# Encoder-layer kernel: the output weights' split moved partly ahead, the hand-off loads reordered, and all weight sums on VectorE

## The chip, the cores and the metric

One Trainium2 chip, of which the kernel uses one core. The metric is the device time of one execution in microseconds (us), lower is better. The trace and the profile come from one profiled execution; all times inside it count from the start of its span.

## The reference, cut to what matters

One encoder layer in float32 on x of 2048 x 1024: an RMS norm, one input projection (1024 to 2304 columns), two kinds of attention, an output projection with a residual, a SwiGLU feed-forward block, a final norm. The change touches the projection, the preparation of the output projection's weights and the start of the attention:

```python
h = rmsnorm(x, g_norm_mix[l])
proj = h @ w_in[l]                       # q, k, v of both kinds of attention
...
oa = neighbourhood_attention(qa, ka, va, na_rpb[l])
ob = windowed_gqa_sink(qb, kb, vb, swa_sink[l])
o = concatenate([rmsnorm(oa, g_out_na[l]), rmsnorm(ob, g_out_swa[l])])
x = x + o @ w_out[l]
```

## The kernel before, in words

**Precision.** A float32 factor is split into two rounded parts, hi (ScalarE, a cast) and lo (VectorE, the value less its hi), and a product is made of three matmuls: hi times hi, hi times lo, lo times hi. Weights and operands must be split before TensorE can use them.

**Stages.** First the tokens are normed and turned and the first 512 value columns are made (up to 116 us). Then comes the product stage, on which the change works: the remaining columns, by a scheme with seven products for a 2 x 2 block product. The tokens are taken in two halves (b = 0, 1) and each half in seven groups of 256 columns; so there are 14 runs g of seven products j, 98 products n = 7g + j, each of 12 matmuls (`product`, L883, lines 910 to 912). The seven operands of the second half (`proj_h_second`, 1 MB each) lie in HBM as sums and are loaded (`load_op`, L315) and split (L563, L729) before run 7.

**Step n.** ScalarE, VectorE and SyncE (SP, which issues most DMAs) each go through steps n = 0 to 99 in a fixed order, written out in tables of steps; each engine works strictly in order, so a wait holds all that is behind it. ScalarE in step n first waits for product n and copies it out where j is 0, 2, 3 (`evacuate`, L577, copy at L590), casts the weights of product n + 6 into a ring of six slots (`pair_hi`, L575), casts an operand where `SPLIT_AT` (L169) says so, then casts finished results into one of three stages (`result_hi`, L602, cast at L618), which first waits for the store that used that stage before. VectorE in step n adds the copied part to the product (`join`, L736, at j = 1, 4, 5), makes the lo parts of the results of step n - 1 (`result_lo`, L775 and L777), turns four results of run 1 and of run 8 by the rotary tables (`rope`, four operations each), makes the lo part of the weight pair (L733) and of the operand (L729). TensorE reads a product's bank pairs by the rules at L883: products j = 2, 4, 5 need ScalarE's copies, j = 6 needs the join of j = 4. Four times (around products 19, 22, 68 and 71) TensorE also turns value results (L880, four transposes each).

**Weight sums.** Each run needs four sums or differences of weight blocks (L453, L455, L459, L464). For runs 1 to 5 VectorE makes them, in steps of the run before (`SUMS_AT` puts the first two of run 1 in step 2); for runs 6 to 13 GpSimd (POOL) does, between its own weight loads (`load_raw`, L466).

**Output weights.** The eight blocks k of `w_out` (512 KB each) are loaded into one buffer (`load_out_weights`), scaled by the group norms' gains and cast (L626, ScalarE), their lo part is made (L782, VectorE), and both parts are stored to HBM (L366, 1 MB). Before, block k is loaded in step 53 + 5k, split in step 55 + 5k and stored after that. The load of block k + 1 waits for the split of block k, since there is one buffer, and the split waits for the store of the block before.

**Operand loads.** In SP's list operand 1 is loaded in step 8 and operand 0 in step 23; they are split in steps 26 and 33. Operands 2 to 6 are loaded by ScalarE's queue in steps 42 to 46.

**Hand-off.** The attention starts with head pair 0 of the neighbourhood kind. Its units u (two heads for each of 16 tiles of queries) go through TensorE (score, L1301; turn, L1313; values, L1336), VectorE (L1248, L1261) and ScalarE (exp, L1200; copy, L1222). Scores 0 to 7 need query portion q0 and key portions k0 and k1; score 8 needs q1 and k2. SP issues q0 in step 91, k0 and k1 in step 93, values v0 and v1 in step 94, the last two mask loads in step 97, and only after the last result's store k2, q1 and the rest (`later_loads`). The results of the last run are numbered r = 52 to 55; r = 55 uses the same stage as r = 52. ScalarE copies no turned unit before the store of r = 53 has landed (`last_stage_stored`, L264). GpSimd makes the bias tables (L1178): kind 0 from masks and `rel` ahead of the hand-off, kinds 1 and 2 once all results are split.

**Banks.** Runs with odd g use PSUM banks 3, 4, 5 (`bank_of`, L178), and the product j = 6 of run 13 ends in bank 3, which the attention's score 3 needs.

The lines quoted are these; the result i of run g is finished in step 7g + `HI_AT`, or 7g + (3, 5, 6, 7) for the runs that it does not name:

```python
    OP_LOADS = {8: 1, 23: 0}
    SPLIT_AT = {26: (1, 1), 33: (1, 0), 46: (1, 2), 48: (1, 3), 49: (1, 4), 51: (1, 5), 52: (1, 6)}
    SUMS_BY_POOL, SUMS_AT = range(6, G), {1: 2}
    HI_AT = {ROPED: (3, 6, 7, 9), VALUES: (3, 7, 6, 9)}
    ROPE_AT = (2, 5, 6, 8)
    OUT_AT = {53 + 5 * k: k for k in range(KT)}
```

## Time and profile before

| | |
|---|---|
| Time, median of 3 runs | 2212.57 us (2206.57 to 2215.93) |
| Profiled execution: its own time | 2212.51 us |
| Profiled execution: span | 2210.7 us |
| Mean granted TensorE clock | 0.992 |
| TensorE (PE) busy | 2147.3 us, 97% |
| VectorE (DVE) busy | 1563.0 us, 71% |
| ScalarE (ACT) busy | 1013.1 us, 46% |
| GpSimd (POOL) busy | 296.1 us, 13% |

The product stage is the stretch from 116.4 to 407.6 us. The shares are means over the whole span; TensorE is near its full share in all stages after 470 us, which this change leaves as they are. Matmuls are pipelined: one shows 0.39 us where the next starts 0.23 us later, so starts say more than durations.

### The profile page before, as it was taken

To read this page: it belongs to the slowest core of one execution; us is meant where nothing else is said; L and a number is where in the kernel's file an instruction comes from. 1 tells how busy PE (TensorE), PEld (TensorE's weight loads), DVE (VectorE), ACT (ScalarE), POOL (GpSimd) and SP (SyncE) were. 2 spreads that over 40 slices of the span, in tenths; PEclk is the share of its full clock that TensorE was granted. 3 is DMA by queue.
4 is the path that set the end of the run, shared out by engine and by line. 5 is a ranking of instruction groups with operands and counts; after the bars stand their busy time and mean duration, and the time that the engine had idled before them with its cause. 6 is when DMAs were issued, how large, how long until landed. Compare 5 with 4: busy or idle time off the path is not lost.

```text
span 2210.7 us, 33085 instructions
## 1 busy us (share of the span) xinstructions
PE 2147.3 (97%) x11168; PEld 1774.7 (80%) x11168; DVE 1563.0 (71%) x2860; ACT 1013.1 (46%) x1967; POOL 296.1 (13%) x307
## 2 busy tenths in 40 slices
PE   7999989699999999999999999999999999999998
PEld 6878767588888888878888888888888887888887
DVE  6776775489888787786656568765656578575676
ACT  5645544388899634353333335333333334131343
POOL 2343432445100000011121211100000000000000
PEclk9999999899999999999999999999999999999999
DMA  6776868999964376565464548332332386353544
GB/s 211 258 236 210 287 216 271 258 265 244 218 195 133 117 237 238 195 223 201 143 213 149 197 165 316 136 124 91 107 108 82 111 321 216 115 185 101 191 148 155
DMA packets 267750, 419.34 MB, mean 190 GB/s; under 512 B 15434, under 2 KB 157266, under 8 KB 261088
## 3 DMA queue, kind: packets, MB, share of 16 engines
q1 hardware_dynamic: 253664, 371.91, 52.3%
q0 software_dynamic: 10240, 30.48, 4.6%
q10 hardware_dynamic: 3712, 15.21, 2.0%
q8 instruction: 79, 1.29, 0.2%
q14 instruction: 55, 0.45, 0.1%
HBM read 264.70 MB, written 156.04 MB: 190 GB/s over the span
## 4 chain that ended last, share of the span: by engine, by line
PE 84%; DVE 6%; DMA 5%; issue 2%; SPq 2%; ACT 1%; DVEq 0%; ACTq 0%
PE late_psum L2393 12%; PE late_psum L2395 12%; PE late_psum L2394 12%; PE late_psum L2419 6%; PE late_psum L2420 6%; PE late_psum L2421 6%; PE late_psum L1336 4%; PE late_psum L1313 3%; PE late_psum L1735 2%; PE late_psum L1737 2%; PE late_psum L1736 2%; PE late_psum L910 2%; PE late_psum L912 2%; PE late_psum L911 2%; PE late_psum L1301 2%
## 5 line engine op out<-in xcount | busy, mean ns | idle before, releaser
L2393 PE MATMUL late_psum<-ff_h,ff_ring 128*128 128x512 f32 x1232 | 479.8, 389 | 1.6 <-DVE ff_acts L2254 1.4
L2394 PE MATMUL late_psum<-ff_h,ff_ring 128*128 128x512 f32 x1232 | 479.3, 389 | 0.0
L2395 PE MATMUL late_psum<-ff_h,ff_ring 128*128 128x512 f32 x1232 | 479.3, 389 | 0.0
L2393 PEld LDWEIGHTS late_psum<-ff_h,ff_ring 128*128 128x128 f32 x1232 | 231.3, 188 | 50.7 <-DVE ff_acts L2254 2.3
L2395 PEld LDWEIGHTS late_psum<-ff_h,ff_ring 128*128 128x128 f32 x1232 | 231.3, 188 | 48.2
L2394 PEld LDWEIGHTS late_psum<-ff_h,ff_ring 128*128 128x128 f32 x1232 | 231.3, 188 | 48.0
L2419 PE MATMUL late_psum<-ff_d,ff_a 128*128 128x512 f32 x616 | 240.1, 390 | 2.1 <-DVE ff_x L2312 1.4
L2421 PE MATMUL late_psum<-ff_d,ff_a 128*128 128x512 f32 x616 | 239.7, 389 | 0.0
L2420 PE MATMUL late_psum<-ff_d,ff_a 128*128 128x512 f32 x616 | 239.7, 389 | 0.0
L2312 DVE TENSOR_TENSOR ff_x<-late_psum,ff_x 128x512 f32<-128x512 f32 x224 | 153.3, 690 | 116.4 <-PE late_psum L2421 115.5
L2212 DVE TENSOR_TENSOR ff_ring<-ff_raw,ff_ring 128x512 fp32r<-128x512 f32 x176 | 131.8, 750 | 99.4 <-ACT ff_ring L2089 99.3
L2104 ACT CAST ff_a<-ff_a 128x768 fp32r<-128x768 f32 (+2 forms) x96 | 81.6, 878 | 206.7 <-DMA ff_a<-acts_scratch 206.5
L2212 DVE TENSOR_TENSOR ff_ring<-ff_sums,ff_ring 128x512 fp32r<-128x512 f32 x132 | 96.1, 729 | 111.6 <-ACT ff_ring L2089 111.2
L2089 ACT CAST ff_ring<-ff_raw 128x512 fp32r<-128x512 f32 x176 | 109.3, 623 | 136.4 <-PE late_psum L2395 135.4
L1200 ACT ACTIVATE att_probs<-att_neg_scores,att_negmax 128x385 f32<-128x385 f32 (+4 forms) x256 | 161.1, 629 | 20.6 <-DVE att_negmax L1248 19.6
L1313 PE MATMUL late_psum<-ident,att_probs 128*128 128x128 f32 (+1 forms) x816 | 133.9, 277 | 8.5 <-ACT att_probs_turned L1222 4.5
L2419 PEld LDWEIGHTS late_psum<-ff_d,ff_a 128*128 128x128 f32 x616 | 115.6, 188 | 27.9 <-issue 2.1
L1222 ACT COPY att_probs_turned<-late_psum 128x384 f32<-128x384 f32 (+2 forms) x256 | 124.5, 487 | 27.1 <-PE late_psum L1313 27.0
L2420 PEld LDWEIGHTS late_psum<-ff_d,ff_a 128*128 128x128 f32 x616 | 115.6, 188 | 23.9
L2421 PEld LDWEIGHTS late_psum<-ff_d,ff_a 128*128 128x128 f32 x616 | 115.6, 188 | 23.8
L2089 ACT CAST ff_ring<-ff_sums 128x512 fp32r<-128x512 f32 x132 | 81.4, 618 | 113.5 <-PE late_psum L2395 110.2
L1301 PE MATMUL late_psum<-att_k_stack,att_q_stack 128*128 128x384 f32 (+3 forms) x256 | 113.0, 441 | 16.5 <-DMA att_q_stack<-qk_scratch 7.7
(208 smaller groups left out, 4142.9 us busy)
## 6 DMA issues: line engine op xcount, KB each, us to landing
acts_scratch<-ff_acts SPq DMA_DIRECT2D x22, 1792.0 KB, 7.7
ff_a<-acts_scratch SPq DMA_DIRECT2D x24, 960.0 KB, 5.1
ff_raw<-in_w_gate SPq DMA_DIRECT2D x44, 512.0 KB, 3.8
ff_raw<-in_w_up SPq DMA_DIRECT2D x44, 512.0 KB, 3.9
att_q_stack<-qk_scratch SPq DMA_DIRECT2D x64, 256.0 KB, 6.4
ff_d<-down_scratch SPq DMA_DIRECT2D x21, 768.0 KB, 6.5
proj_raw<-in_w_in POOLq DMA_DIRECT2D x14, 1024.0 KB, 9.5
ffn_in_scratch<-mix_h_stage SPq DMA_DIRECT2D x8, 1792.0 KB, 6.3
```

What stands on the lines that cost most here:

```text
L1200: nc.scalar.activation(pr[:, i, lo:hi], sn[:, i, lo:hi], ACT.Exp, bias=negmax[:, i:i + 1], scale=-1.0, accum_out=total[:, i:i + 1]).then_i ...
L1301: pe.matmul(out, q, kind.keys(k_st[:, e, 0, :], t), start=True, stop=False)
L1313: last = pe.transpose(tp[0:rows, u % 2, j * P:(j + 1) * P], pr[:, i, c0 + j * P:c0 + j * P + rows], ident[:])
L2089: nc.scalar.copy(ff.ring[m % TURNS][:, 0], weight_of(m)).then_inc(w_hi_done, 1)
L2212: nc.vector.tensor_tensor(ff.ring[m % TURNS][:, 1], weight_of(m), ff.ring[m % TURNS][:, 0], ALU.subtract) \
L2312: nc.vector.tensor_tensor(to, down_bank(e, j), to, ALU.add).then_inc(added, 1)
L2393: pe.matmul(out_bank, whi[:, k], hhi[:, :, k], start=(k == 0 and not onto), stop=False, skip_group_check=onto)
L2394: pe.matmul(out_bank, whi[:, k], hlo[:, :, k], start=False, stop=False, skip_group_check=onto)
L2395: last = pe.matmul(out_bank, wlo[:, k], hhi[:, :, k], start=False, stop=(k == 3), skip_group_check=onto)
L2419: pe.matmul(bank, hi, dhi, start=(i == 0 and not onto), stop=False, skip_group_check=onto)
L2420: pe.matmul(bank, hi, dlo, start=False, stop=False, skip_group_check=onto)
L2421: last = pe.matmul(bank, lo, dhi, start=False, stop=(i == n - 1), skip_group_check=onto)
```

## The change

- The output weights are split in two groups of four. Blocks 0 to 3 are loaded in steps 14, 15, 19, 25, split in steps 18, 23, 28, 32; blocks 4 to 7 are loaded in steps 51, 53, 58, 63 and split in steps 57, 62, 67, 72. Each half has two raw buffers and one buffer for the parts. The first half's buffers lie in the home of operand 1, so that operand's load moves from step 8 to step 36 and waits for the fourth store; its split moves from step 26 to step 40. Operand 0's load moves from step 23 to step 21.
- All weight sums are made by VectorE. The first two of run 1 move to step 4, the third to step 5, and weight pairs 7 to 12 each come one step later.
- Odd runs use banks 5, 4, 3 where they used 3, 4, 5; score 3 now waits for the last join, and turn 1 for the last result.
- Results r = 52 and 53 get two stages of their own, in the buffer of the weights of even runs.
- The masks and `rel` are loaded in steps 77 to 85. In the hand-off SP issues q0 in step 92, k1 in step 94, v0 and v1 in step 95, k2 and q1 in step 96; ScalarE's queue issues k0 in step 93. v2, k3, q2, q3 and v3 stay behind the last store.

```diff
@@ -161,22 +162,22 @@
         return hs[:, o] if t >= 8 else op_sums(0, o)[:, quarter(t)]
-    SPLIT_ORDER = [(0, o) for o in (2, 3, 4, 6)] + [(1, o) for o in (1, 0, 2, 3, 4, 5, 6)]
-    OP_LOADS = {8: 1, 23: 0}
+    SPLIT_ORDER = [(0, o) for o in (2, 3, 4, 6)] + [(1, o) for o in range(SEVEN)]
+    OP_LOADS = {21: 0, 36: 1}
     LATE_OPS, OP_SLOTS = PER_G * HALF_GROUPS - PER_G - 2, range(2, SEVEN)
...
     PAIR_AT_TILE = {11: 0, 12: 1, 13: 2}
-    SPLIT_AT = {26: (1, 1), 33: (1, 0), 46: (1, 2), 48: (1, 3), 49: (1, 4), 51: (1, 5), 52: (1, 6)}
-    SUMS_BY_POOL, SUMS_AT = range(6, G), {1: 2}
+    SPLIT_AT = {33: (1, 0), 40: (1, 1), 46: (1, 2), 48: (1, 3), 49: (1, 4), 51: (1, 5), 52: (1, 6)}
+    SUMS_BY_POOL, SUMS_AT = (), {1: 4}
     PAIRS_AT = {n: (n + RING,) for n in range(PRODUCTS - RING)}
-    PAIRS_AT.update({0: (4, 5, 6), 1: (), 2: (), 3: (7,), 4: (8, 9), 5: (10, 11)})
+    PAIRS_AT.update({0: (4, 5, 6), 1: (), 2: (), 3: (), 4: (7, 8), 5: (9, 10), 6: (11, 12)})
     HOME_FREED = {o: PER_G * HALF_GROUPS - PER_G + o - 1 for o in range(2, SEVEN)}
...
     def bank_of(g, j):
-        return ps[:, 3 * (g % 2) + BANK_OF[j]]
+        return ps[:, 5 - BANK_OF[j] if g % 2 else BANK_OF[j]]
     def weight_of(n):
...
@@ -216,6 +218,10 @@
...
         stored_by[r] = (stored_by[r - STAGES] if r >= STAGES else 0) + (16 if is_value(g, i) else 32)
+    def stage_of(r):
+
+        return {LAST_RUN: STAGES, LAST_RUN + 1: STAGES + 1}.get(r, r % STAGES)
+
     def results_at(n):
...
@@ -247,10 +253,13 @@
...
         else:
+            eng.wait_ge(summed, 3 * G)
+
+    def turns_free(eng, u):
+        if u == 0:
+            eng.wait_ge(summed, 3 * G)
+        else:
             eng.wait_ge(res_lo, LOWS)
-
-    def turns_free(eng):
-        eng.wait_ge(summed, 3 * G)
     def last_turn_read(eng):
...
@@ -317,6 +323,8 @@
...
             eng.wait_ge(h_stored, 128)
+            if o == 1:
+                eng.wait_ge(out_stored, 64)
         if o == 0:
...
@@ -346,51 +354,71 @@
...
                 to = qk_dram[part, r0:r0 + P, cols]
-            sp.dma_start(to, src).then_inc(stored[slot], 16)
+            sp.dma_start(to, src).then_inc(landed, 16)
     def load_out_weights(k):
         if k == 0:
+            sp.wait_ge(parts_stored, 128)
+            sp.wait_ge(h_stored, 128)
+        elif k in (4, 5):
             sp.wait_ge(prod_done, PER_G * HALF_GROUPS)
-        else:
-            sp.wait_ge(out_lo_done, k)
+        elif k >= 2:
+            sp.wait_ge(out_lo_done, k - 1)
+        raw_rows = out_raw[k // 4][k % 2]
         if k < 4:
-            sp.dma_start(out_raw[:], w_out[k * P:(k + 1) * P, :]).then_inc(out_in, 32)
+            sp.dma_start(raw_rows[:], w_out[k * P:(k + 1) * P, :]).then_inc(out_in[k % 2], 32)
             return
...
             r0 = AW + (k - 4 + 4 * e) * HD
-            sp.dma_start(out_raw[e * HD:(e + 1) * HD, :], w_out[r0:r0 + HD, :]).then_inc(out_in, 16)
+            sp.dma_start(raw_rows[e * HD:(e + 1) * HD, :], w_out[r0:r0 + HD, :]).then_inc(out_in[k % 2], 16)
     def store_out_weights(k):
         sp.wait_ge(out_lo_done, k + 1)
-        sp.dma_start(out_dram[k], out_parts[:].bitcast(F32)).then_inc(out_stored, 16)
-
-    OUT_AT = {53 + 5 * k: k for k in range(KT)}
+        sp.dma_start(out_dram[k], out_parts[k // 4][:].bitcast(F32)).then_inc(out_stored, 16)
+
+    OUT_LOAD_AT = {14: 0, 15: 1, 19: 2, 25: 3, 51: 4, 53: 5, 58: 6, 63: 7}
+    OUT_AT = {18: 0, 23: 1, 28: 2, 32: 3, 57: 4, 62: 5, 67: 6, 72: 7}
+
+    NEAR_AT = {77: 3, 79: 4, 81: 0, 83: 1, 85: 2}
     def load_near(part):
+        if part == 3:
+            out_weights_stored(sp)
+        if part == 0:
+            sp.wait_ge(roped, 8)
+            sp.wait_ge(v_turned, 4)
+            sp.wait_ge(table_made, 16 * (2 + 8 * NAH))
         dst, src = near_parts[part]
-        sp.dma_start(dst, src).then_inc(near_in if part < 3 else near_masks_in, 16)
+        sp.dma_start(dst, src).then_inc(near_in, 16)
+
+    FIRST_AT = {92: 0, 94: 2, 95: 3, 96: 4}
     def first_loads(att, turn):
-        sp.wait_ge(prod_done, PRODUCTS - SEVEN + (1, 3, 4)[turn])
+        eng = act if turn == 1 else sp
+        eng.wait_ge(prod_done, PRODUCTS - SEVEN + (1, 3, 3, 4, 4)[turn])
         if turn == 0:
...
         if turn == 1:
-            att.load_k(att.near, 0, 0)
+            for slot in range(STAGES):
+                act.wait_ge(stored[slot], max(v for r, v in stored_by.items() if r % STAGES == slot and order[r][1] < G - 2))
+            att.load_k(att.near, 0, 0, act)
+        if turn == 2:
             att.load_k(att.near, 0, 1)
-        if turn == 2:
+        if turn == 3:
             for half in range(2):
...
             att.load_v(att.near, 0, 1)
+        if turn == 4:
+            att.load_k(att.near, 0, 2)
+            att.load_q(att.near, 0, 1)
     def later_loads(att):
-        att.load_k(att.near, 0, 2)
-        att.load_q(att.near, 0, 1)
         att.load_v(att.near, 0, 2)
...
@@ -416,29 +444,16 @@
...
                 load_op(sp, OP_LOADS[n])
-            if n in OUT_AT:
-                load_out_weights(OUT_AT[n])
-            if n - 2 in OUT_AT:
-                store_out_weights(OUT_AT[n - 2])
-            if n == 78:
-                sp.wait_ge(roped, 8)
-                sp.wait_ge(v_turned, 4)
-                sp.wait_ge(table_made, 16 * (2 + 8 * NAH))
-                load_near(0)
-            if n in (83, 87):
-                load_near({83: 1, 87: 2}[n])
+            if n in OUT_LOAD_AT:
+                load_out_weights(OUT_LOAD_AT[n])
+            if n - 1 in OUT_AT:
+                store_out_weights(OUT_AT[n - 1])
+            if n in NEAR_AT:
+                load_near(NEAR_AT[n])
+            if n in FIRST_AT:
+                first_loads(att, FIRST_AT[n])
             for r, g, i in results_at(n - 1):
                 store_result(r, g, i)
-            if n == 91:
-                first_loads(att, 0)
-            if n == 93:
-                first_loads(att, 1)
-            if n == 94:
-                first_loads(att, 2)
-            if n == 97:
-                out_weights_stored(sp)
-                for part in (3, 4):
-                    load_near(part)
         later_loads(att)
...
@@ -600,10 +615,12 @@
...
     def result_hi(r, g, i):
-        slot, kind = r % STAGES, res_kind(g, i)
-        if r >= STAGES:
-            act.wait_ge(stored[slot], stored_by[r - STAGES])
-        elif slot == 2:
+        slot, kind = stage_of(r), res_kind(g, i)
+        if STAGES <= r < LAST_RUN + STAGES:
+            act.wait_ge(stored[r % STAGES], stored_by[r - STAGES])
+        if r == LAST_RUN:
+            act.wait_ge(w_lo_done, PER_G * (G - 1))
+        if r == 2:
             for half in range(2):
...
@@ -620,12 +637,12 @@
...
             act.wait_ge(gains_in, 48)
-        act.wait_ge(out_in, 32 * (k + 1))
+        act.wait_ge(out_in[k % 2], 32 * (k // 2 + 1))
         if k >= 1:
             act.wait_ge(out_stored, 16 * k)
-        nc.scalar.mul(out_parts[:, 0], out_raw[:], gains[:, k:k + 1]).then_inc(out_hi_done, 1)
-
-    def scalar():
+        nc.scalar.mul(out_parts[k // 4][:, 0], out_raw[k // 4][k % 2][:], gains[:, k:k + 1]).then_inc(out_hi_done, 1)
+
+    def scalar(att):
         load_x(0)
...
@@ -831,12 +851,12 @@
...
                     first_weight_sums(dve, g + 1)
-                if j == 2:
+                if n == (5 if g == 0 else PER_G * g + 2):
                     middle_weight_sum(dve, g + 1)
...
                     last_weight_sum(dve, g + 1)
-            if n - 2 in OUT_AT:
-                out_weights_lo(OUT_AT[n - 2])
+            if n in OUT_AT:
+                out_weights_lo(OUT_AT[n])
     def turn_tile(n):
...
@@ -1304,8 +1324,8 @@
...
         c0, _, _ = kind.score_cols(t)
-        if u == 0 and isinstance(r, int) and r == 0:
-            proj.turns_free(pe)
+        if u < 2 and isinstance(r, int) and r == 0:
+            proj.turns_free(pe, u)
         pe.wait_ge(probs_done, UNITS * r + u + 1)
...
@@ -1409,7 +1429,7 @@
...
         self.p_sums = self.at("proj_w_sums", 207872, [P, 2, 4, P])
-        stages = (24576, 28672, 180224)
+        stages = (24576, 28672, 180224, 199680, 203776)
         self.p_st_hi = [self.at(f"stage_hi{i}", off, [P, BANK], F32R) for i, off in enumerate(stages)]
...
@@ -1417,8 +1437,9 @@
...
         self.p_spare = [self.at(f"proj_spare{b}", off, [P, BANK]) for b, off in enumerate((75776, 55296))]
-        self.p_out_raw = self.at("w_out_raw", 32768, [P, D])
-        self.p_out_parts = self.at("w_out_parts", 36864, [P, 2, D], F32R)
+        self.p_out_raw = [[self.at(f"w_out_raw{half}_{i}", off, [P, D]) for i, off in enumerate(offs)]
+                          for half, offs in enumerate(((81920, 94208), (32768, 61440)))]
+        self.p_out_parts = [self.at(f"w_out_parts{half}", off, [P, 2, D], F32R) for half, off in enumerate((86016, 36864))]
         self.ident = self.at("ident", self.IDENT, [P, P])
```

## Rows read from the trace of the kernel before

**Rows 1.** Busy by stretch: length, busy PE PEld DVE ACT POOL (instructions), PEclk, DMA share, GB/s

```profile
116.44:407.60 291.16, 274.82 (x1193) 223.21 (x1191) 195.12 (x264) 131.79 (x213) 109.94 (x119) 0.98 0.76 244
...
407.60:431.46 23.86, 7.12 (x25) 5.67 (x26) 9.54 (x31) 8.92 (x22) 10.03 (x9) 0.67 1.05 293
...
137.46:164.66 27.20, 27.20 (x122) 22.52 (x120) 23.83 (x42) 10.10 (x18) 9.79 (x17) 1.00 0.72 230
```

**Rows 2.** Timeline of TensorE: first matmuls of six products: start, us, engine, line

```profile
116.44 0.39 PE L910 MATMUL late_psum<-proj_h_first,proj_ring 128*128 128x512 f32 x1
...
119.16 0.39 PE L910 MATMUL late_psum<-proj_h_first,proj_ring 128*128 128x512 f32 x1
...
134.62 0.47 PE L910 MATMUL late_psum<-proj_h_first_last,proj_ring 128*128 128x512 f32 x1 [1.70 <-issue]
...
269.66 0.50 PE L910 MATMUL late_psum<-proj_h_second,proj_ring 128*128 128x512 f32 x1 [1.59 <-DVE proj_h_second L729]
...
307.19 0.80 PE L910 MATMUL late_psum<-proj_h_second,proj_ring 128*128 128x512 f32 x1 [6.59 <-ACT proj_c L590]
...
365.08 0.79 PE L910 MATMUL late_psum<-proj_h_second,proj_ring 128*128 128x512 f32 x1 [2.51 <-DVE proj_c L742]
```

**Rows 3.** Chain of waits, products 19 to 21: start us, us, what

```profile
173.73 0.44 PE late_psum L880 x4
```

**Rows 4.** Waits, 237 to 408 us: who waited for what: total us, times, longest

```profile
ACT w_out_parts L626 <- DMA w_out_raw<-in_w_out: 17.0, 5, 9.7
...
ACT stage_hi L618 <- DMA qk_scratch<-stage_lo: 8.5, 4, 6.8
```

**Rows 5.** Chain of waits from the last product to the ninth score

```profile
408.80 8.20 DMA qk_scratch<-stage_lo
...
417.02 0.61 ACT stage_hi L618
...
424.05 7.18 DMA att_q_stack<-qk_scratch
...
431.46 0.76 PE late_psum L1301
```

**Rows 6.** Timeline around the hand-off: SP's queue, VectorE, GpSimd and ScalarE

```profile
399.05 5.54 SPq L1107 DMA_DIRECT2D att_k_stack<-qk_scratch  x8
...
418.26 0.51 DVE L1248 CUSTOM_DVE_ANT_0 att_neg_scores<-late_psum,bias 128x352 f32<-128x352 f32 x1
...
419.61 3.75 SPq L1107 DMA_DIRECT2D att_k_stack<-qk_scratch  x4
...
421.43 13.62 POOL L1178 TENSOR_TENSOR bias<-near_mask,rel 128x512 f32<-128x512 f32 x12 [25.48 <-DMA near_mask<-in_na_mask]
...
423.53 0.59 ACT L1200 ACTIVATE att_probs<-att_neg_scores,att_negmax 128x352 f32<-128x352 f32 x1 [0.44 <-DVE att_negmax L1248]
...
432.81 0.66 DVE L1248 CUSTOM_DVE_ANT_0 att_neg_scores<-late_psum,bias 128x480 f32<-128x480 f32 x1 [5.85 <-PE late_psum L1302]
```

**Rows 7.** VectorE's groups: by tile, 116 to 200, 237 to 408, 116 to 408 us

```profile
L729 DVE TENSOR_TENSOR proj_h_second<-proj_h_second x7: 2278/2292/3244, 196.3 to 270.1; 128x2048 fp32r<-128x2048 f32 x7
...
L733 DVE TENSOR_TENSOR proj_ring<-proj_raw,proj_ring 128x512 fp32r<-128x512 f32 x17 | 11.6, 687 | 4.5 <-ACT proj_ring L575 4.5
...
L733 DVE TENSOR_TENSOR proj_ring<-proj_raw,proj_ring 128x512 fp32r<-128x512 f32 x29 | 27.7, 966 | 8.0 <-ACT proj_ring L575 8.0
...
L782 DVE SCALAR_TENSOR_TENSOR w_out_parts<-w_out_raw,g_out,w_out_parts 128x1024 fp32r<-128x1024 f32 x8 | 10.3, 1293 | 22.0 <-ACT w_out_parts L626 22.0
...
L464 DVE TENSOR_TENSOR proj_w_sums<-proj_raw,proj_w_sums 128x512 f32<-128x512 f32 x6 | 4.1, 686 | 0.0
```

**Rows 8.** DMA times to landing: second-half operand loads, then output-weight stores

```profile
DMA to landing us min/median/max: 6.1/10.9/14.0
...
DMA to landing us min/median/max: 3.9/5.3/12.1
```

**Rows 9.** DMA traffic from 392 to 442 us

```profile
DMA packets 8887, 13.48 MB, mean 270 GB/s; under 512 B 681, under 2 KB 4137, under 8 KB 8758
```

More of the change, by code:

```diff
@@ L781, in out_weights_lo @@
         dve.wait_ge(out_hi_done, k + 1)
[L782 to L783 removed]
+        parts = out_parts[k // 4]
+        nc.vector.scalar_tensor_tensor(out=parts[:, 1], in0=out_raw[k // 4][k % 2][:], scalar=gains[:, k:k + 1],
+                                       in1=parts[:, 0], op0=ALU.mult, op1=ALU.subtract).then_inc(out_lo_done, 1)
     def vector():
```

35 lines of the change are left out of this document (17 added, 18 removed).

## The prediction

> **What bounds the kernel now.** I read busy time by stretch first [rows 1]. In the product stage (116.44 to 407.60 us) TensorE shows 274.82 us busy of 291.16, in the 23.86 us after it only 7.12. So the change works in two places in which TensorE does wait. How much is lost in the first? Two undisturbed products start 2.72 us apart (116.44 and 119.16) [rows 2]; 98 of them are 266.6 us, and four turns of values at 0.44 us [rows 3] are 1.8. So 291.2 - 266.6 - 1.8 = 22.8 us of the product stage are stall. Its large pieces [rows 2]: product 6 starts at 134.62 where 116.44 + 6 x 2.72 = 132.76 was due; product 54 waits 1.59 for VectorE's operand part; product 65 waits 6.59 for ScalarE's copy and product 83 waits 2.51 for VectorE's join. Both resume at half the clock (0.80 and 0.79 us for a matmul, where 0.39 is usual), which makes them dearer than the idle alone.
>
> Who holds ScalarE and VectorE? ScalarE waited 17.0 us for the output weights' loads, 9.7 the longest, and 8.5 us for stores out of the result stages [rows 4]; the 9.7 is the wait that ends just ahead of product 65. In the hand-off the chain runs over a stage store of 8.20 us from 408.80 (r = 52, whose stage r = 55 wants), the last result's hi part at 417.02, then SP's later issues and q1's landing of 7.18 us, to score 8 at 431.46 [rows 5], 23.9 us after the product stage.
>
> **First part: output weights, steps 14 to 72.** Each load now starts four to nine steps ahead of its split (11 to 24 us) where it was two steps (5.4 us). The longest wait now comes 9.7 us on top of those 5.4, so a load needs up to 15 us; the tightest of the second half (step 51 for 57) has 16, and block 0's (step 14 for 18) has some 19, since SP has nothing to issue in steps 12 and 13 and comes to it early. I take the waits behind products 65 and 83 as gone, and with them the small ones that follow a late ScalarE. In the first half the same four splits are new work: 4 x 1.29 us on VectorE [rows 7], where TensorE ran without a gap from 137.46 to 164.66 with VectorE 23.83 of 27.20 us busy [rows 1]; the later steps 18 to 32 have no rotary work, so I cost them at nothing. If that cover is gone the price is 5.2 us.
>
> Operand 1's load is the delicate move. Its issue waits in SP's list for the fourth store. Let product 33 start at P. The fourth split ends at P + 2.5 and its store lands 5.3 us later, 12.1 at most [rows 8]; step 36 itself comes at about P + 10. So the load goes out at P + 10 to P + 15 and takes 10.9 us (6.1 to 14.0) [rows 8]: P + 16 to P + 28.6, likeliest P + 21. Its split comes up at P + 21.8 (step 40). The next copy that TensorE needs from ScalarE is product 42's, due at P + 29.9, with 3.1 us of work before it. So 5 us of lateness cost nothing, and the worst case loses 2. Operand 0's load in step 21 waits for the value turn after product 22 as it did, and now holds the stores of steps 20 and 21 behind it; ScalarE meets that in step 24, after its copies of that run: nothing, or 2 us.
>
> **Second part: weight sums on VectorE.** GpSimd's operations stretch VectorE's: the weights' lo part took 0.687 us up to 200 us and 0.966 from 237 to 408, 29 times, 8.1 us in all; an operand part took 3.24 instead of 2.29 [rows 7]. That ends. In exchange VectorE gets 32 operations of 0.69 us [rows 7], 22 us over eight runs of 19 us. Is there room? The stretch of 27.20 us has 42 instructions in 23.83 us busy, four of them empty, so 0.63 each. A run needs 3 joins, 4 lo parts, 7 pairs and 4 sums, 18 x 0.63 = 11.3 us. Over steps 42 to 69 (76.2 us) that is 45.4, with five operand parts 11.5, four rotary turns 10.1 and three output parts 3.9: 70.9 us, 93%. It fits on the whole, not in steps 46 to 52, where 11.3 + 11.5 = 22.8 us meet 19.0. Laid out step by step, VectorE ends operand 6's part and the join of product 53 some 7 us after product 53's start, and product 55 is due 5.4 after it; product 54 is 0.4 late. So products 54 and 55 lose 2.0 us, where product 54's idle alone is 1.59 now. In the rotary steps 58 to 64 the same layout has VectorE some 5 us behind its steps, with the join for product 69 just late: 0.8.
>
> **Third part: start of the product stage.** VectorE sat in the sums of run 1 until the weights landed, with the join for product 6 behind it. Moved to step 4, the join goes first: 1.9 us back.
>
> The product stage: 22.8 us of stall, of which I leave 2.0 + 0.8 and 2.5 for landings (operand loads, stage stores of the first half): 5.3. **Gain 17.5 us**, between 8 (all the new costs above) and 22.
>
> **Fourth part: hand-off.** Call the stage's end T. With two more stages r = 55 waits for no store: its parts are made by T + 1.3, and scoring can start, given k1. SP issues k1 when product 93 is done, T - 10.9; four issues took 2.8 us (half of 5.54 [rows 6]) and a landing 7 to 8 us [rows 5], so about T. Units 0 to 7 took VectorE from 418.26 to 432.81 less 5.85 idle, 8.7 us [rows 6], so unit 8 could be shifted at T + 10.2; it was at T + 25.2. GpSimd's bias kind 1 is the first half of 13.62 us [rows 6] and starts at about T + 1.5: no later than that. But ScalarE waits for r = 53's store before unit 0's copy and exp 5, and SP now issues k2 and q1 (3.75 us for k2 [rows 6]) ahead of it. Bytes bound this: 13.48 MB went at 270 GB/s from 392 to 442 us [rows 9]. From T - 15 to that store there are four stores, q0, k0, k1, v0, v1, k2, q1 and r = 53: 6.75 MB, 25 us, so T + 10 if nothing pauses. I take T + 11. From exp 5 to unit 8's shift the trace has 9.28 us with 5.85 idle [rows 6], 3.4; unit 8 at T + 14.4. **Gain 11 us**, between 4 and 15.
>
> The rule that speaks against this part is in the Trainium skill, DMA: Bandwidth & Descriptors, Issuing engines are not separate DMA queues: transfers from all engines run on the same 16 DMA engines, so k0 on ScalarE's queue would save issue time only. By that rule the sum would count 2.8 us of issue for k0 and nothing for its landing.
>
> **Sum.** 2212.51 (the profiled execution, as good as the median 2212.57) - 17.5 - 11 = 2184.0 us. All later stages only move, since TensorE, VectorE and ScalarE meet the same work in the same order there.
>
> **Rivals.** (a) The hand-off is bound by transfers: the DMA share is 1.05 there [rows 1], and packing the same bytes closer makes each landing longer: with pauses before the loads of T - 10.9 and T - 8.2, the 25 us count from T - 6, and unit 8 comes at T + 22. Then 3 us are gained: 2192. For it speaks the full share; against it, that the masks and the last output-weight store (2.3 MB, 8.6 us at 270 GB/s) leave the stretch. (b) VectorE bounds steps 42 to 69: at its records' 0.69 us instead of 0.63, the 88 short operations there take 5.3 us more and fill the 76.2 us, and two stalls with half-clock restarts add some 3. Then the stage gains 8 us less: 2192. Against it speaks the full 27.20 us at 88% busy. (c) Slower: ScalarE, in order, now meets loads in the first half where it met none, four output-weight blocks and two operands. One such wait of 9.7 us cost product 65 some 8 us (6.59 idle and matmuls at half the clock). It decides from the fourth wait of that length on; all six cost 49 us and give 2212.5 + 49 - 28.5 = 2233. Against it: 15 us and more from issue to want for the blocks, 12 for the operands. (d) Both (a) and (b), or the gains are given back at once: 2202 to 2212.
>
> **Chances.** Forecast 0.60, (a) 0.16, (b) 0.14, (c) 0.03, (d) 0.07. A measurement of this kernel can tell about 0.5%, 11 us. Faster by more: 0.60 + 0.16 + 0.14 and 0.01 of (d), 0.91; within 0.5%: the other 0.06 of (d); slower: 0.03. The range takes the forecast's bounds (12 to 37 us of gain, 2175 to 2200) and both single rivals: 2174 to 2200.
>
> **What would show it.** Right: no wait of ScalarE for output weights, product 65 on time, the weights' lo part back at 0.69 us, TensorE's product stage near 274 us long, unit 8 shifted 13 to 16 us after it, last result's hi part within 1 us of the last product. Wrong: ScalarE waiting at step 18 or 40 for a load; TensorE idle for VectorE's joins in products 54 to 69 by more than 4 us; score 8 or 16 waiting for q1, k2 or q2 beyond T + 15. A span above 2200 would make the prediction wrong.

## The result, and the profile after

| | before | after |
|---|---|---|
| Time, median of 4 runs | 2212.31 us | 2198.21 us (2197.29 to 2200.47) |
| Ratio | | 0.994, 95% interval 0.9917 to 0.9963 |
| Profiled execution: its own time | 2212.51 us | 2197.36 us |
| Profiled execution: span | 2210.7 us | 2195.2 us |
| End of the product stage (T) | 407.4 us | 400.3 us |
| From T to the end | 1803.3 us | 1795.0 us |

The change gains 14.1 us where 28.5 were forecast. The time lies inside the range, but the gain is half of the forecast. T is read here as 0.23 us after the start of the last product's last matmul. The last two lines of the table split the 15.5 us between the two profiled executions: 7.1 us in the product stage (forecast 17.5) and 8.3 us behind it (forecast 11).

Busy time by stretch of the changed kernel: the product stage, the 23.86 us after it, and the first runs [rows 1].

```profile
116.01:400.25 284.24, 274.45 (x1193) 224.87 (x1191) 203.18 (x296) 131.83 (x212) 57.24 (x87) 0.98 0.80 257
400.25:424.11 23.86, 14.72 (x101) 11.71 (x102) 16.57 (x56) 15.19 (x39) 13.66 (x12) 0.79 1.08 277
136.00:163.20 27.20, 27.20 (x122) 22.53 (x121) 25.19 (x44) 11.79 (x21) 10.36 (x18) 1.00 0.73 218
```

The stage is 284.2 us long, so by the prediction's own count 284.2 - 266.6 - 1.8 = 15.8 us of stall are left, where 5.3 were forecast. TensorE does twice as much as before in the 23.86 us after it.

TensorE's timeline, first matmuls of product 30 (203.35), 51 (266.72) and 65 (308.98) of the changed kernel:

```profile
203.35 0.80 PE L930 MATMUL late_psum<-proj_h_first,proj_ring 128*128 128x512 f32 x1 [4.60 <-ACT proj_c L605]
...
266.72 0.63 PE L930 MATMUL late_psum<-proj_h_second,proj_ring 128*128 128x512 f32 x1 [3.39 <-issue]
...
308.98 0.50 PE L930 MATMUL late_psum<-proj_h_second,proj_ring 128*128 128x512 f32 x1 [0.19 <-ACT proj_c L605]
```

Product 65 is on time, as forecast, and so are 6 and 83. But two products that ran without a gap before are now late. "Loss" from here on is the time by which the matmuls of a product start later than one per 0.227 us: the gap ahead of it plus its slow matmuls, read from the starts. Product 30 loses 4.8 + 2.4 us and its successor 0.3, product 51 loses 3.6 + 1.7: 12.7 us in all. That is more than the 10.5 us by which the stall exceeds the 5.3 that the forecast left; the 3.1 us of stall besides it are less than 5.3.

Waits of ScalarE from 110 to 402 us, changed kernel, then the same row of the kernel before:

```profile
ACT stage_hi L635 <- DMA qk_scratch<-stage_lo: 25.8, 8, 11.5
```

```profile
ACT stage_hi L618 <- DMA qk_scratch<-stage_lo: 13.5, 6, 6.8
```

No wait for an output weight's load is left, and 0.8 us of wait for an output weight's store [rows 4]. The wait for a stage's store has doubled instead, and one of them is 11.5 us long. ScalarE and the chain of waits around it, changed kernel:

```profile
197.84 0.63 ACT L635 ACTIVATE stage_hi<-proj_c 128x512 fp32r<-128x512 f32 x1 [11.49 <-DMA qk_scratch<-stage_lo]
...
202.73 0.56 ACT L605 COPY proj_c<-late_psum 128x512 f32<-128x512 f32 x1
```

```profile
180.77 17.05 DMA qk_scratch<-stage_lo
...
197.84 0.64 ACT stage_hi L635
```

A store of 256 KB issued at 180.77 took 17.05 us to land. ScalarE stood at L635 for it, with the copy for product 30 behind it in its order.

The hand-off [rows 5, 6]: the chain that leads to score 16, then ScalarE and VectorE.

```profile
407.39 4.86 SPq L1127
...
415.79 12.64 DMA att_q_stack<-qk_scratch
...
428.54 0.48 PE late_psum L1321
```

```profile
413.68 0.48 ACT L1242 COPY att_probs_turned<-late_psum 128x384 f32<-128x384 f32 x1 [5.83 <-DMA qk_scratch<-stage_lo]
...
416.44 0.63 DVE L1268 CUSTOM_DVE_ANT_0 att_neg_scores<-late_psum,bias 128x480 f32<-128x480 f32 x1
```

ScalarE's first copy waits for r = 53's store, until T + 13.4 (forecast T + 11). Unit u is timed by the start of its first VectorE operation, in which its scores are shifted (L1268). Unit 8 is shifted at T + 16.2 (forecast T + 14.4, before T + 25.4). Unit 16 comes at T + 29.2, because score 16 needs q2, whose last part SP issues at 415.79 and which takes 12.64 us to land, at T + 28.2. The prediction had named this as a sign of being wrong: "score 8 or 16 waiting for q1, k2 or q2 beyond T + 15".

VectorE's groups, changed kernel, weight lo parts (L752) from 237 to 400 us and one kind of weight sum [rows 7]:

```profile
L752 DVE TENSOR_TENSOR proj_ring<-proj_raw,proj_ring 128x512 fp32r<-128x512 f32 x30 | 21.3, 714 | 12.5 <-ACT proj_ring L590 12.5
...
L468 DVE TENSOR_TENSOR proj_w_sums<-proj_raw 128x512 f32<-128x512 f32 x9 | 6.2, 686 | 0.0
```

The lo part is back at 0.71 us from 0.97.

### The profile page after: what moved, and what is told of

It is laid out like the page before. It is cut to its first block, busy times and chain, and to the rows that moved or that the text cites. A ratio compares the mean times of both kernels' runs of the same rounds, so it can differ in the third digit from the quotient of the medians.

```text
span 2195.2 us, 33087 instructions
## 1 busy us (share of the span) xinstructions
PE 2144.0 (98%) x11168; PEld 1775.8 (81%) x11168; DVE 1569.1 (71%) x2892; ACT 1012.1 (46%) x1967; POOL 245.0 (11%) x275
## 4 chain that ended last, share of the span: by engine, by line
PE 86%; DVE 5%; DMA 4%; issue 2%; ACT 1%; SPq 1%; DVEq 0%; ACTq 0%
PE late_psum L2414 12%; PE late_psum L2415 12%; PE late_psum L2416 12%; PE late_psum L2440 6%; PE late_psum L2442 6%; PE late_psum L2441 6%; PE late_psum L1356 4%; PE late_psum L1333 3%; PE late_psum L930 3%; PE late_psum L932 3%; PE late_psum L931 3%; PE late_psum L1756 3%; PE late_psum L1758 3%; PE late_psum L1757 3%; PE late_psum L1321 2%
## 5 line engine op out<-in xcount | busy, mean ns | idle before, releaser
L2233 DVE TENSOR_TENSOR ff_ring<-ff_raw,ff_ring 128x512 fp32r<-128x512 f32 x176 | 131.1, 746 | 102.4 <-ACT ff_ring L2110 102.3
L1220 ACT ACTIVATE att_probs<-att_neg_scores,att_negmax 128x385 f32<-128x385 f32 (+4 forms) x256 | 161.2, 630 | 19.6 <-DVE att_negmax L1268 18.8
L1333 PEld LDWEIGHTS late_psum<-ident,att_probs 128*128 128x128 f32 (+1 forms) x816 | 98.4, 139 | 43.5 <-issue 24.8
```

Of the source, the lines that this page charges most:

```text
L1220: nc.scalar.activation(pr[:, i, lo:hi], sn[:, i, lo:hi], ACT.Exp, bias=negmax[:, i:i + 1], scale=-1.0, accum_out=total[:, i:i + 1]).then_i ...
L1333: last = pe.transpose(tp[0:rows, u % 2, j * P:(j + 1) * P], pr[:, i, c0 + j * P:c0 + j * P + rows], ident[:])
L2233: nc.vector.tensor_tensor(ff.ring[m % TURNS][:, 1], weight_of(m), ff.ring[m % TURNS][:, 0], ALU.subtract) \
```

## The experiments

Each edit is to the changed kernel unless it says otherwise. Single executions are compared by their stages in the trace; kernels with the changed hand-off differ by up to 5 us from T to the end (1792 to 1797), so differences below that are not read as effects there. Nor are small differences in time: except where a median is given each time is of one execution, and the kernel before took 2210.48 us beside the first four edits, 2208.31 beside the next four, 2209.6 (median of nine) beside the three after them and 2209.97 beside the last two.

**Operand 0's load later.**

```diff
-    OP_LOADS = {21: 0, 36: 1}
+    OP_LOADS = {23: 0, 36: 1}
```

> The changed kernel with operand 0's load back in step 23. In the changed kernel's trace product 30 stands still for 4.8 us and restarts at half the clock (7.1 us lost in all), behind a result store of step 20 that took 17 us to land: SP had held it until product 22's value turn and then issued it just behind the 1 MB operand load. Theory A (order in SP's list): the store goes out in step 21 again, ahead of the load, the stall at product 30 is gone, and the time falls by about 7 us, to some 2191. Theory B (the output weights' new traffic in the first half slows the stores whatever the order): the stall stays within 2 us of what it is, the time stays at 2198.

2199.94 us. Product 30 still loses 5.3 + 1.8 us, product 51 still 6.4. A place two steps later in SP's list does not remove the first stall (Theory B). ScalarE's timeline now has other, shorter waits for stores ahead of it:

```profile
195.04 0.63 ACT L635 ACTIVATE stage_hi<-proj_c 128x512 fp32r<-128x512 f32 x1 [7.87 <-DMA qk_scratch<-stage_lo]
...
202.73 0.63 ACT L635 ACTIVATE stage_hi<-proj_c 128x512 fp32r<-128x512 f32 x1 [3.23 <-DMA v_window_scratch<-stage_values]
```

The second of them is released just before the copy at 203.27, and it waits for a value store. So the lateness is not one store's alone.

**Operand 1's split one step earlier.**

```diff
-    OP_LOADS = {21: 0, 36: 1}
-    SPLIT_AT = {33: (1, 0), 40: (1, 1), ...
+    OP_LOADS = {23: 0, 36: 1}
+    SPLIT_AT = {33: (1, 0), 39: (1, 1), ...
```

> As the run before, and operand 1 split in step 39 instead of 40. The changed kernel loses 5.2 us at product 51, where ScalarE waits for stores of steps 41 and 42 that were issued among the five operand loads of steps 42 to 46 and took 16 to 18 us to land. Theory A (the operand split in step 40, 1.9 us on ScalarE and 2.3 on VectorE, pushes those stores behind the loads): stores of steps 40 and 41 go out some 2 us earlier and the loss at product 51 falls by 2 us or more; time some 3 to 5 us under the run before, about 2187. Theory B (VectorE is late there from the weight sums, or the loads alone fill the transfer engines): the loss at product 51 changes by less than 1 us.

2196.12 us. Product 51 loses 0.1 where it lost 5.2, product 30 still loses 6.3, products 54 and 55 lose 3.8 instead of 2.1. T is 396.7. The stall goes as Theory A says; the time does not reach its 2187, which counted on a smaller stall at product 30. So product 51's stall hangs on the split in step 40. The changed kernel's SP shows how:

```profile
234.84 0.33 SPq L357 DMA_DIRECT2D qk_scratch<-stage_hi  x1
...
242.24 0.33 SPq L357 DMA_DIRECT2D qk_scratch<-stage_hi  x1
...
247.48 0.45 SPq L357 DMA_DIRECT2D qk_scratch<-stage_lo  x1
```

and its ScalarE queue and ScalarE:

```profile
241.87 0.35 ACTq L334 DMA_DIRECT2D proj_h_second<-proj_in_scratch  x1
...
259.88 0.63 ACT L635 ACTIVATE stage_hi<-proj_c 128x512 fp32r<-128x512 f32 x1 [3.96 <-DMA qk_scratch<-stage_lo]
...
265.52 0.63 ACT L635 ACTIVATE stage_hi<-proj_c 128x512 fp32r<-128x512 f32 x1 [2.68 <-DMA qk_scratch<-stage_lo]
```

Step 40 has results to split too. With 1.9 + 2.3 us of operand split in it, the result stores of steps 40 to 42 go out 1.4 to 4.0 us later than before, counted from product 43's start, and so behind the 1 MB operand loads that begin at 241.87. The store issued at 247.48 landed 18.0 us later, at 265.5, where ScalarE stands at L635 ahead of product 51's copy.

**Only r = 50 awaited at the end.** ScalarE's first copy then waits for r = 50's store instead of r = 53's, which has a stage of its own now.

```diff
-        eng.wait_ge(stored[2], max(v for r, v in stored_by.items() if r % STAGES == 2))
+        eng.wait_ge(stored[2], max(v for r, v in stored_by.items() if stage_of(r) == 2))
```

> The changed kernel with one wait narrowed: ahead of the first copy of a turned unit ScalarE waits for the last store out of stage 2 (now r = 50), not for the store of r = 53, which has moved to a stage of its own. In the changed kernel ScalarE waits 5.8 us there, and unit 8 is shifted 16.2 us after the product stage's end T. Theory A (that wait holds the hand-off): ScalarE's wait goes, unit 8 comes at T + 10 to 12, and 2 to 5 us stay to the end, 2193 to 2196. Theory B (transfers bound the first round anyway): unit 8 comes earlier but by unit 64 less than 1 us is left, and the time stays at 2198.

2197.61 us. Unit 8 comes 4.3 us earlier (T + 11.9), unit 16 is as late as before at T + 29.3, and the end at T + 1795.0. The wait that sets unit 8 is not the one that sets the stage (Theory B). q2 takes it all back: SP issues its last part at 414.58, it takes 13.74 us to land, and score 16 starts at T + 28.0:

```profile
414.58 13.74 DMA att_q_stack<-qk_scratch
428.32 0.12 issue
428.44 0.76 PE late_psum L1321
```

**Sums on GpSimd again.**

```diff
-    SUMS_BY_POOL, SUMS_AT = (), {1: 4}
+    SUMS_BY_POOL, SUMS_AT = range(6, G), {1: 4}
```

> The changed kernel with the weight sums of runs 6 to 13 given back to GpSimd. Theory A (the sums on VectorE are worth what the contention cost, and have nothing to do with product 51): the weights' lo part beside GpSimd goes back to some 0.97 us in the mean from 240 to 400 us, the stall at product 51 stays, and 2 to 4 us are lost at products 53 to 55 and 67 to 79: 2200 to 2202. Theory B (VectorE's extra work makes the stall at product 51): that stall falls by over 3 us, and the time is 2195 or less.

2195.03 us, T at 400.0 (400.3 in the changed kernel). The time and the stall are as Theory B says: product 51 loses 1.6 us where it lost 5.2, and the result stores of steps 40 to 42 go out 0.6 to 1.4 us earlier, counted from product 43's start. So the sums on VectorE have a part in the stall at product 51. Slower operations give some of it back: 4.7 us are lost at products 54, 55, 65 and 67 together, where the changed kernel loses 2.6. Products 30 and 31 lose 1.0 more, in a stretch that the edit leaves alone. The move of the sums to VectorE is worth nothing in the changed kernel; with operand 1 split in step 39, where product 51 loses nothing anyway, it was not undone.

**Bias tables later.** GpSimd builds the bias table in HBM by 16 small transfers in each of runs 2 to 5. Here they go with runs 6, 7, 9 and 10, with the split in step 39.

```diff
-            if g < 6:
-                bias_rows(2 * (g - 2))
+            if g in (6, 7, 9, 10):
+                bias_rows(2 * (6, 7, 9, 10).index(g))
```

> The changed kernel with operand 1 split in step 39, and GpSimd's 64 small loads of the bias table (rows of 192 bytes) issued after its weight loads of runs 6, 7, 9 and 10 in place of runs 2 to 5. The stall at product 30 stayed when the operand load went back to step 23, so the order in SP's list is not its cause. Theory A (the first half's transfers are too many while the table is being made: output-weight loads and stores, an operand, weights and 48 small table loads between 163 and 200 us): the stores of steps 20 to 23 land within 10 us, and the loss at product 30 (6 to 7 us) falls below 2 us; the product stage's end comes at about 391 us. Theory B (the table's small transfers do not matter, the 1 MB transfers ahead of the stores in SP's own queue do): the loss at product 30 stays over 5 us.

2196.97 us, T at 398.2. Product 30 loses nothing, as Theory A says. But T was to be 391: another stall has come, products 65 and 66 lose 7.4 us. TensorE there, and GpSimd's queue:

```profile
304.69 0.80 PE L930 MATMUL late_psum<-proj_h_second,proj_ring 128*128 128x512 f32 x1 [4.47 <-ACT proj_c L605]
```

```profile
259.95 8.94 POOL L496 DMA_DIRECT2D rel_scratch<-pad_scratch  x16
...
280.74 8.94 POOL L496 DMA_DIRECT2D rel_scratch<-pad_scratch  x16
```

ScalarE's longest wait near it is 4.4 us for an output-weight store. Tables beside output weights stall a product in this run's second half as they did in the first; the runs below show that it depends on where they are put.

**Operand 0's load in step 27**, split in step 39, tables as in the changed kernel.

```diff
-    OP_LOADS = {21: 0, 36: 1}
+    OP_LOADS = {27: 0, 36: 1}
```

> The changed kernel with operand 1 split in step 39, and operand 0's load in step 27 in place of 21, behind the stores of steps 20 to 26. Theory A (too many bytes between 172 and 200 us, of which this load is 1 MB): ScalarE's wait for the store of step 21 ends some 4 us sooner, and the loss at product 30 falls by 3 us or more, unless the split in step 33 then waits for the load. Theory B (the output weights' own 1 MB stores and 0.5 MB loads are enough to hold the result stores): the loss stays within 2 us of 7.

2190.57 us. Product 30 loses 1.5, product 37 loses 4.0, T is 396.3. Theory A holds at product 30, but it is not the amount of traffic that fell: from 165 to 205 us this run moves 12.05 MB with 31 table transfers, the changed kernel 11.69 MB with 30. What changed is that the 1 MB load now goes out behind the result stores; a part of the stall moves with it.

**The start alone, on the kernel before**: the sums of run 1 in steps 4 and 5, weight pairs 7 to 12 a step later.

```diff
-    SUMS_BY_POOL, SUMS_AT = range(6, G), {1: 2}
+    SUMS_BY_POOL, SUMS_AT = range(6, G), {1: 4}
-    PAIRS_AT.update({0: (4, 5, 6), 1: (), 2: (), 3: (7,), 4: (8, 9), 5: (10, 11)})
+    PAIRS_AT.update({0: (4, 5, 6), 1: (), 2: (), 3: (), 4: (7, 8), 5: (9, 10), 6: (11, 12)})
```

> The kernel before with the start of the change alone (first sums of run 1 in step 4, the third in step 5, weight pairs 7 to 12 a step later). Theory A: product 6 starts on time, 1.9 to 2.1 us are gained there and all of it is kept at the product stage's end (405.3 us in place of 407.4). Theory B: the gain is given back at the store waits around product 18 or at product 65, whose load does not start earlier: the product stage ends within 0.5 us of before.

2209.21 us, beside 2208.31 for the kernel before: the time shows no gain. Product 6 is on time and T is 1.8 us earlier (Theory A), and unit 8 is at T + 25.0 (before T + 25.4).

**The hand-off alone, on the kernel before**: two more stages, turned banks and the new load order, but masks and output weights where they were.

```diff
+    FIRST_AT = {92: 0, 94: 2, 95: 3, 96: 4}
-        slot = r % STAGES
+        slot, landed = stage_of(r), stored[r % STAGES]
-        stages = (24576, 28672, 180224)
+        stages = (24576, 28672, 180224, 199680, 203776)
```

> The kernel before with the hand-off of the change alone (two more stages, banks turned round, k0 from ScalarE's queue, k1, k2 and q1 ahead of the last stores), the masks and the last output weights left where they were. Theory A (the reordering is worth what the change showed): unit 8 is shifted at T + 16 to 18 and unit 64 7 us earlier than in the kernel before, T + 96 to 97. Theory B (transfers bound the hand-off, and what helped was that masks and an output-weight store left the stretch): unit 64 comes at T + 100 or later, and less than 4 us are gained.

2209.25 us, beside 2208.31 for the kernel before; unit 0 is 4.6 us earlier, unit 8 at T + 26.4 where it was at T + 25.4, unit 64 at T + 102.4 where it was at T + 103.5, the end at T + 1801.6 (Theory B). GpSimd and VectorE of this kernel:

```profile
424.38 13.94 POOL L1193 TENSOR_TENSOR bias<-near_mask,rel 128x512 f32<-128x512 f32 x12 [30.22 <-DMA near_mask<-in_na_mask]
```

```profile
432.00 0.66 DVE L1263 CUSTOM_DVE_ANT_0 att_neg_scores<-late_psum,bias 128x480 f32<-128x480 f32 x1 [8.28 <-POOL bias L1193]
```

With q1 and k2 ahead of them in SP's list, the masks land later than before [rows 6], the bias of kind 1 starts at T + 18.8, and unit 8 waits for that instead of for q1.

**What was found, taken together.** Operand 0 in step 27, the split in step 39, tables in runs 2, 3, 7 and 12; beside it the changed kernel once more, both timed against the same runs of before.

```diff
+    OP_LOADS = {27: 0, 36: 1}
+    SPLIT_AT = {33: (1, 0), 39: (1, 1), ...
+            if g in (2, 3, 7, 12):
+                bias_rows(2 * (2, 3, 7, 12).index(g))
```

> The changed kernel with what the earlier runs found taken together: operand 0's load in step 27, operand 1's split in step 39, and the bias tables' small transfers in runs 2, 3, 7 and 12 instead of 2 to 5. Theory A (the small table transfers of runs 4 and 5 and operand 1's split in step 40 are the two causes of the new stalls, and each can be removed by itself): products 30, 37 and 51 lose under 1.5 us together where products 30, 51 lost 12.6 in the changed kernel; the product stage ends at 391 to 394, and the time is 2185 to 2190. Theory B (the tables collide wherever they are put, as in the run with them in runs 6, 7, 9 and 10): a stall of over 4 us stands at another product, most likely 37 to 44 or 74 to 80, and the time stays at 2191 to 2196.

> The changed kernel itself once more, on the same chip and against the same runs of before as the kernel with the parts taken together, for the size of the gain and of what separates the two. Both theories: 2196 to 2200, a ratio of 0.993 to 0.997 to before; stalls at products 30 and 51 of 5 to 8 us each.

| | median | ratio to before (2209.6 us) | 95% interval |
|---|---|---|---|
| taken together | 2187.47 us | 0.9904 | 0.9888 to 0.9919 |
| changed kernel again | 2197.99 us | 0.9949 | 0.9935 to 0.9962 |

Theory A holds: products 30, 37 and 51 lose 0.1 us together; 54 loses 4.0. The stage ends at 390.2. Its stretch, and ScalarE's wait for stores in it:

```profile
116.11:390.21 274.10, 271.28 (x1193) 222.77 (x1191) 201.78 (x296) 131.58 (x212) 56.84 (x87) 0.99 0.83 267
```

```profile
ACT stage_hi L635 <- DMA qk_scratch<-stage_lo: 11.3, 7, 4.1
```

DMA from 165 to 205 us, changed kernel and then this one:

```profile
DMA packets 5094, 11.69 MB, mean 292 GB/s; under 512 B 802, under 2 KB 1826, under 8 KB 4709
## 3 DMA queue, kind: packets, MB, share of 16 engines
q1 hardware_dynamic: 3540, 8.06, 55.9%
q0 software_dynamic: 1553, 3.61, 33.4%
...
rel_scratch<-pad_scratch POOLq DMA_DIRECT2D x30, 48.0 KB, 7.0
```

```profile
DMA packets 4618, 11.96 MB, mean 299 GB/s; under 512 B 338, under 2 KB 1362, under 8 KB 4185
## 3 DMA queue, kind: packets, MB, share of 16 engines
q1 hardware_dynamic: 3821, 8.87, 63.0%
q0 software_dynamic: 796, 3.08, 24.5%
```

More bytes pass in the same 40 us with far shorter waits. The bytes alone do not make the stall.

**The load order alone undone.** All loads by SP, q0 in step 91, k0 and k1 in 93, v0 and v1 in 94, k2 and q1 behind the last store.

```diff
-    FIRST_AT = {92: 0, 94: 2, 95: 3, 96: 4}
+    FIRST_AT = {91: (0,), 93: (1, 2), 94: (3,)}
```

> The changed kernel with the hand-off loads back in the old order and steps, all issued by SP (q0 in step 91, k0 and k1 in 93, v0 and v1 in 94, k2 and q1 behind the last store); the masks, the two stages and the banks stay as changed. The product stage should end at 400.3 as in the changed kernel. Theory A (what helped the hand-off is that the masks and the last output-weight store have left it): unit 8 of the attention is shifted within 2 us of the changed kernel's T + 16.2 and unit 64 within 2 us of T + 96.2; the time is 2196 to 2200. Theory B (the new order of the loads made the gain): unit 8 comes at T + 20 or later, unit 64 at T + 100 or later, and the time is 2202 to 2206.

2194.74 us: unit 8 at T + 16.4, unit 64 at T + 93.2, the end at T + 1791.3. The new order brings nothing (Theory A).

**The masks late.** The changed kernel with the mask loads of 768 and 576 KB in step 97, as before.

```diff
-    NEAR_AT = {77: 3, 79: 4, 81: 0, 83: 1, 85: 2}
+    NEAR_AT = {81: 0, 83: 1, 85: 2}
+            if n == 97:
+                for part in (3, 4):
+                    load_near(part)
...
```

> The changed kernel with the last two mask loads (768 and 576 KB) back behind the last run's results, in step 97, where the kernel before had them. Theory A (what helped the hand-off is the transfers that left it: 1.38 MB of masks, 5.1 us at 270 GB/s, and the last output-weight store of 1 MB, 3.9 us): unit 8 is shifted at T + 19 to T + 22 where the changed kernel had T + 16.2, or unit 64 at T + 99 to T + 102 where it had T + 96, and the time is 2200 to 2204. Theory B (the two stages for the last results and the turned banks made the gain, and the masks are hidden): unit 8 within 1.5 us of T + 16.2, unit 64 within 2 us of T + 96.2, time 2195 to 2199.

2202.72 us: unit 8 at T + 22.9, unit 64 at T + 100.6, the end at T + 1800.0. That is 5.0 us later than in the changed kernel and 2.8 later than in the latest of its like (T + 1797.2), so 3 to 5 us of the 8.3 are lost. VectorE, and the GpSimd group that it waits for:

```profile
423.46 0.66 DVE L1274 CUSTOM_DVE_ANT_0 att_neg_scores<-late_psum,bias 128x480 f32<-128x480 f32 x1 [8.13 <-POOL bias L1204]
```

```profile
415.85 13.92 POOL L1204 TENSOR_TENSOR bias<-near_mask,rel 128x512 f32<-128x512 f32 x12 [35.87 <-DMA near_mask<-in_na_mask]
```

In the changed kernel the same group starts at T + 2.3:

```profile
402.58 13.66 POOL L1198 TENSOR_TENSOR bias<-near_mask,rel 128x512 f32<-128x512 f32 x12 [22.91 <-DVE stage_lo L796]
```

**The whole old hand-off, with early masks.** All loads by SP in the old order and steps, three stages and the old banks.

```diff
-        return {LAST_RUN: STAGES, LAST_RUN + 1: STAGES + 1}.get(r, r % STAGES)
+        return r % STAGES
-        return ps[:, 5 - BANK_OF[j] if g % 2 else BANK_OF[j]]
+        return ps[:, 3 * (g % 2) + BANK_OF[j]]
```

> The changed kernel with the whole hand-off as it was before (old load order and steps, three stages, old banks), and only the masks and the output weights early. Theory A (transfers that left): unit 8 at T + 16 to T + 19, unit 64 at T + 94 to T + 99, the end 1792 to 1798 after T, time 2193 to 2199. Theory B (stages and banks): the last result's hi part waits for the store of r = 52 again, unit 8 at T + 22 or later and the end 1800 or more after T, time 2200 to 2205.

2198.71 us: unit 8 at T + 17.9, unit 64 at T + 95.3, the end at T + 1793.1, no later than in the changed kernel. Its product stage ends 3.6 us later (403.8): it starts 0.6 later, product 30 loses 1.6 more and the rest is small losses. That makes its time. The chain, to set beside [rows 5]:

```profile
401.06 6.58 DMA qk_scratch<-stage_lo
407.66 0.61 ACT stage_hi L627
...
413.12 7.02 DMA att_q_stack<-qk_scratch
```

The chain is that of the kernel before, link by link: r = 52's store, the last hi part, SP's issues, q1. But the store goes out 2.7 us before T, where it went at T + 1.4, and lands 1.6 us faster; the last hi part is made at T + 3.9 instead of T + 9.6.

Why so late before? SP's queue in the kernel before, from 370 to 430 us: what SP waited for, and two of its issues.

```profile
SPq L366 <- DVE w_out_parts L782: 12.4, 2, 6.9
...
392.23 0.33 SPq L366 DMA_DIRECT2D w_out_scratch<-w_out_parts  x1
...
396.59 1.30 SPq L1097 DMA_DIRECT2D att_q_stack<-qk_scratch  x2
```

SP stood 6.9 us for the last output weight's lo part, until T - 15.2, with the hand-off's stores and loads behind it in its order, and then issued without a pause: it reached q0 at T - 10.8 and k0 at T - 8.3, where this kernel's SP reached them at T - 15.5 and T - 10.7. The old place of the masks has no part in that, since SP issues them at T + 5.1, after r = 52's store; in the store's longer landing it may.

## Why the prediction was wrong by half

**The range and the sign were right.** The time of 2198.2 us lies in 2174 to 2200, near its end; the likeliest case was wrong. Rivals (a) and (b) gave 2192 with other causes, and (c) gave a slower kernel by a wait of the same kind as the one that did occur.

**Failed: the first half's output weights "at nothing".** I said that steps 18 to 32 "have no rotary work, so I cost them at nothing". That looked at VectorE only, and there the split was free. What it cost was in DMA. From 165 to 205 us 9.19 MB passed before and 11.69 MB after, in both with some 30 small table transfers among them, and a 256 KB store that ScalarE needs took 17.05 us. Products 30 and 31 lost 7.5 us. I had seen the mechanism as rival (c), "ScalarE, in order, now meets loads in the first half", with the very price (a product loses some 8 us), but looked for it at the output-weight and operand loads. Those came in time. It was the stage stores beside them that came late, and the 2.5 us that I left "for landings" were a third of it. The kernel before had the tables without the output weights, and the run with late tables the output weights without most of the tables; product 30 lost nothing in either, so both are needed for the stall. The third part is where operand 0's load stands: in step 27 it leaves 1.5 us.

**Failed: operand 1's split in step 40.** I worked out when its load would land (P + 21 for a split at P + 21.8) and what ScalarE owed to product 42. The load was no problem: it was issued at 225.57, half a microsecond behind a store. I did not ask what the split itself pushes back, which were the result stores of that step, past the operand loads. Cost 5.2 us at product 51; a step earlier it is 0.1, and 1.7 more are lost at 54 and 55. The sums that the change gave VectorE share in it: with them on GpSimd the same split costs 1.6. The sum's 2.5 us for landings stood where the two new stalls measured 12.7. The count of VectorE's room missed a price too. It looked for late joins in steps 46 to 52, and what came late first were the result stores of steps 40 to 42.

**Right:** product 6 (1.9 forecast; 1.98 less loss there, T 1.8 earlier with it alone), products 65 and 83 on time (12.4 us of loss before, 0.5 after), the last result's hi part made without a wait, from T + 0.7 on. Products 53 to 55 lose 2.1 (forecast 2.0), but that was luck: TensorE's stall at product 51 gives VectorE time to catch up just before, and in the runs without it products 54 and 55 lose 3.8 to 4.0, while where product 51 loses 6.3 (operand 0's load in step 23) product 54 loses 0.1.

**Without gain: the sums.** The lo part did come back to 0.71 us, but with the sums on GpSimd the stage is as long. The exchange of 8.1 us of stretching for 22 us of work was worth nothing here: it spared 2.1 us at products 54 to 67 and cost 3.7 at product 51. Rival (b) was right that VectorE's load matters in these steps, though by stores that go out late and not by joins.

**The hand-off: size nearly right, reason wrong.** I credited two stages, the new order and the turned banks. With all three undone the end comes as early after T; with all three alone it comes at most 2 us earlier. The gain is that of the masks (3 to 5 us), and of what else had left the stretch: the last output weight, with its 1 MB store and SP's wait of 6.9 us for its lo part. No run undid its place alone, so its share, and how it divides between bytes and SP's wait, stays open. I had put the transfers down only as a reason against rival (a), and SP's wait not at all. I also left out q2: score 16 waits for it until T + 28.2, and the run that waits only for r = 50 shows that it, and not unit 8, sets how far the attention has come by then. And the sentence that the bias of kind 1 starts "at about T + 1.5: no later than that" was right (T + 2.3), but I passed over what makes it so: it waits for the masks, [rows 6], 25.48 us before the change. In the kernel before both were late: this bias started at T + 14.1 and q1 landed at T + 23.9. The new order cures the second and early masks the first. With masks and output weights early and the old order, q1 lands at T + 16.3: SP reaches k0 2.4 us earlier, and its issues and the store's landing are shorter.

**The rule weighed.** By the Trainium skill, DMA: Bandwidth & Descriptors, Issuing engines are not separate DMA queues, k0 on ScalarE's queue should save issue time only. The undone order, with SP issuing k0, lost nothing at all. That agrees with what the rule says for the landing; the 2.8 us of issue don't show either. No run moved k0 alone. That the first score could start earlier mattered little, as the run that waits only for r = 50 shows: 4.3 us at unit 8 were nothing by unit 16.

**Open.** Why product 54 loses 4.0 us in the best kernel wasn't tried, nor which of its three edits could be left out, nor what the sums on VectorE are worth in it.

## What to carry to other kernels

When a step is moved into an idle-looking stretch, cost its bytes by what they do to the landings of the stores that an in-order engine waits for there, and cost its engine time by the stores that it pushes back past the next large loads. In an overlap between two stages, list what every late unit waits for, on all engines, before crediting an order of loads. A wait removed early in a stage is worth only what is left of it when the next late transfer is met.

## What was unexpected on this hardware

- Small transfers are somewhat dear beyond their bytes. From 165 to 205 us GpSimd's queue has no table transfers in the best kernel and takes 24.5 / 3.08 = 8.0 points of share for a megabyte, SP's 63.0 / 8.87 = 7.1. In the changed kernel 30 tables of 48 KB (1.5 MB) are among GpSimd's 3.61 MB. If the other 2.1 MB cost 8.0 each, the tables took the remaining 16 points, by this estimate 11 for a megabyte.
- Two stores of 256 KB took 17 to 18 us to land, the first with the mean at 292 GB/s around it, where those on the hand-off's chains landed in 6.6 and 8.2. The mean rate does not tell such landings: with 299 GB/s in the best kernel ScalarE's longest wait for one was 4.1 us.
